# Attention in a decoder layer: two query tiles share an output bank, and ScalarE copies the output weights

## What is computed

```python
z = jnp.einsum('bhqd,bhkd->bhqk', qi, kf) * scale
causal = key_pos[None, :] < q_pos[:, None]
log_1m_beta = jnp.where(causal, jax.nn.log_sigmoid(-z), 0.0)
stick = lax.cumsum(log_1m_beta, axis=3, reverse=True) - log_1m_beta
a = jnp.where(causal, jnp.exp(jax.nn.log_sigmoid(z) + stick), 0.0)
return jnp.einsum('bhqk,bhkd->bhqd', a, vf)
```

## Time and profile before

| | us |
|---|---|
| median of three runs | 2598.17 |
| the profiled execution | 2601.36 |
| its span | 2599.7 |
| attention, from the first scores to the last addition | 435.1 to 945 |
| busy in the whole span: PE, DVE, ACT, POOL | 2402.9, 1651.4, 1229.3, 737.2 |

### The profile page before, as it was taken

One profiled execution on the slowest core, in us unless ns is written; L12 is line 12 of the kernel. 1 busy time (PEld: TensorE's weight loads), 2 busy tenths in 40 slices (PEclk: granted clock), 3 DMA queues, 4 the chain that ended last, 5 costly groups with the idle time before them and its releaser, 6 DMA issues. The chain is left out here.

```text
span 2599.7 us, 38083 instructions
## 1 busy us (share of the span) xinstructions
PE 2402.9 (92%) x11925; PEld 2004.6 (77%) x11925; DVE 1651.4 (64%) x2100; ACT 1229.3 (47%) x2065; POOL 737.2 (28%) x624
## 2 busy tenths in 40 slices
PE   6989997989999979985999999799999899999997
PEld 5767885878888868873888888688888687878785
DVE  4424222989999967865777777877777634343433
ACT  4311112879898955544444444544444324232322
POOL 0000001776666634554222222222222001010101
PEclk9999998999999989997999999899999999999998
DMA  7922335243343125774322223432222254545452
GB/s 238 285 72 80 129 121 147 70 125 98 93 98 89 45 86 176 230 226 155 98 73 92 77 79 109 145 96 74 85 84 73 80 180 148 191 142 194 149 194 105
DMA packets 283122, 326.90 MB, mean 126 GB/s; under 512 B 11972, under 2 KB 217468, under 8 KB 278396
## 3 DMA queue, kind: packets, MB, share of 16 engines
q1 hardware_dynamic: 278396, 308.68, 39.0%
q0 software_dynamic: 4608, 16.78, 1.6%
HBM read 216.36 MB, written 92.27 MB: 119 GB/s over the span
## 5 line engine op out<-in xcount | busy, mean ns | idle before, releaser
L747 POOL TENSOR_TENSOR weight<-beta,stick 128x512 f32<-128x512 f32 (+3 forms) x320 | 304.2, 958 | 586.4 <-ACT beta L696 467.3
L794 DVE TENSOR_TENSOR_SCAN stick<-z_ps,stick,beta 128x512 f32<-128x512 f32 x192 | 245.1, 1276 | 13.8 <-ACT z_ps L697 12.7
L511 PE MATMUL out_ps<-hT,w_hi 128*128 128x512 f32 x768 | 239.5, 393 | 10.0 <-DVE w_lo L445 10.0
L1638 PE MATMUL value_chain_ps<-wide,wu_hi 128*128 128x512 f32 x704 | 219.9, 394 | 16.8 <-DVE up_cols L1587 9.7
L696 ACT ACTIVATE beta<-z_ps 128x512 f32<-128x512 f32 (+3 forms) x320 | 171.1, 535 | 70.7 <-PE z_ps L828 61.1
L1418 ACT ACTIVATE wu_hi<-wu_sums 128x512 fp32r<-128x512 f32 x175 | 110.4, 633 | 186.9 <-PE value_chain_ps L1638 93.0
L1755 POOL TENSOR_TENSOR y<-y,x 128x1024 f32<-128x1024 f32 x16 | 38.9, 2432 | 505.6 <-DVE y L1814 505.4
L845 PE MATMUL wT_ps<-ident,weight 128*128 128x128 f32 x1088 | 174.7, 276 | 5.7 <-POOL weight L747 5.7
L511 PEld LDWEIGHTS out_ps<-hT,w_hi 128*128 128x128 f32 x768 | 144.9, 189 | 42.1 <-DVE w_lo L445 10.4
L697 ACT ACTIVATE z_ps<-z_ps 128x512 f32<-128x512 f32 (+3 forms) x320 | 172.2, 538 | 0.0
L1638 PEld LDWEIGHTS value_chain_ps<-wide,wu_hi 128*128 128x128 f32 x704 | 133.8, 191 | 45.9 <-DVE wu_lo L1515 10.0
(11 more groups left out here) (210 smaller groups left out, 6236.8 us busy)
## 6 DMA issues: line engine op xcount, KB each, us to landing
wu_f<-in_w_down SPq DMA_DIRECT2D x88, 512.0 KB, 3.6
wu_f<-in_w_up SPq DMA_DIRECT2D x44, 512.0 KB, 5.0
bridge<-in_w_up SPq DMA_DIRECT2D x44, 512.0 KB, 5.0
f_scratch<-f SPq DMA_DIRECT2D x44, 512.0 KB, 2.6
wu_sums<-f_scratch SPq DMA_DIRECT2D x88, 256.0 KB, 3.8
x_scratch<-x SPq DMA_DIRECT2D x56, 256.0 KB, 2.6
xt<-in_x SPq DMA_DIRECT2D x16, 512.0 KB, 5.8
hT<-h_hi SPq DMA_DIRECT2D x16, 512.0 KB, 4.5
```

The source lines that it names most:

```text
L511: m = pe.matmul(out_ps[half + j][:, :], w[slot][:, k, :], hT[h][:, k, j * BANK:(j + 1) * BANK], start=(k == 0 and t == 0), stop=(k == kc - ...
L747: pool.tensor_tensor(weight[v % weight_ring][:, 0:w], beta[v % stick_in][:, 0:w], stick[q % 2][:, at:at + w], ALU.mult).then_inc(weight_do ...
L794: dve.tensor_tensor_scan(stick[q % 2][:, at:at + w][:, ::-1], backwards, beta[u % stick_in][:, 0:w], start, ALU.mult, ALU.bypass).then_inc ...
L1638: m = pe.matmul(bank[:, :], w[left][:, k, :], x[right][:, k, :], start=(not adds and k == 0 and t == 0), stop=(k == half - 1 and t == 2), ...
```

## The change

The two output buffers get twice the width, 128 x 2 x 2 x 128, which is a whole bank each: one buffer holds two neighbouring query tiles. PE asks for a free buffer only at even tiles, counted in pairs, and DVE adds only after odd tiles, with one instruction that reads 512 elements and writes 256. The wait for the stored `mixed` of the pair of heads before moves from tile 0 to tile 1. SP counts 8 additions in a head in place of 16.

`high_wo` goes from DVE to ACT and becomes an activation with the function Copy, at the head of the step, ahead of the two sigmoids. `wo_part` now gives units 8, 12, ..., 68 of the first pair, for ACT and for POOL's `low_wo`, which stays the same otherwise. SP's code for the weights is not changed.

```diff
-        o_ps = [n.ps(f"o_ps{i}", [P, 2, P]) for i in range(2)]
+        o_ps = [n.ps(f"o_ps{i}", [P, 2, 2, P]) for i in range(2)]
...
         def wo_part(i, u):
-            m = (u - per_head) // 2
-            return m if isinstance(i, int) and i == 0 and (u - per_head) % 2 == 0 and 0 <= m < 2 * a["kc"] else None
+            m = (u - lead) // 4
+            return m if isinstance(i, int) and i == 0 and (u - lead) % 4 == 0 and 0 <= m < 2 * a["kc"] else None
...
-                    sp.wait_ge(o_read, done((pair * 2 + e + 1) * tiles - 1, lead))
+                    sp.wait_ge(o_read, done((pair * 2 + e + 1) * (tiles // 2) - 1, lead))
...
+                def high_wo(m):
+                    k, h = m // 2, m % 2
+                    act.wait_ge(wo_in[h], 16 * (k + 1))
+                    act.activation(wide[h][:, k, :], wo_f[:, h, :], ACT.Copy).then_inc(wo_hi_done, 1)
                 def step(i, u, behind):
+                    if wo_part(i, u) is not None:
+                        high_wo(wo_part(i, u))
                     if u < total:
...
-                def high_wo(m):
-                    k, h = m // 2, m % 2
-                    dve.wait_ge(wo_in[h], 16 * (k + 1))
-                    dve.tensor_copy(wide[h][:, k, :], wo_f[:, h, :]).then_inc(wo_hi_done, 1)
                 def step(i, u, behind):
-                    if wo_part(i, u) is not None:
-                        high_wo(wo_part(i, u))
...
-                    if behind(read_lag) and units[behind(read_lag)[0]][5]:
+                    if behind(read_lag) and units[behind(read_lag)[0]][5] and units[behind(read_lag)[0]][1] % 2 == 1:
...
-                        if q == 0:
+                        if q == 1:
                             dve.wait_ge(mixed_out[e], stored(i if u >= read_lag else i - 1, 32))
-                        dve.tensor_reduce(mixed[e][:, q * P:(q + 1) * P], o_ps[q % 2][:, :, :].rearrange("e h k -> e k h"), AX.X,
-                                          ALU.add).then_inc(o_read, 1)
+                        dve.tensor_reduce(mixed[e][:, (q - 1) * P:(q + 1) * P].rearrange("e (q k) -> e q k", q=2),
+                                          o_ps[q // 2 % 2][:, :, :, :].rearrange("e q h k -> e q k h"), AX.X, ALU.add).then_inc(o_read, 1)
...
-                    if first:
-                        pe.wait_ge(o_read, freed(i * (2 * tiles) + (e * tiles + q), 2, lead))
+                    if first and q % 2 == 0:
+                        pe.wait_ge(o_read, freed(i * tiles + (e * (tiles // 2) + q // 2), 2, lead))
```

More of the change, by code:

```diff
@@ L854, in values @@
                         for b in range(per):
-                            m = pe.matmul(o_ps[q % 2][:, 0, :], v_f[:, key // P + b, :, :], wT_f[whole_before[u] % wT_ring][:, b, :],
+                            m = pe.matmul(o_ps[q // 2 % 2][:, q % 2, 0, :], v_f[:, key // P + b, :, :], wT_f[whole_before[u] % wT_ring][:, b, :],
                                           start=False, stop=False, skip_group_check=True)
@@ L861, in values @@
                     closes = last or (key == BANK and whole[u + 1])
-                    if first:
-                        pe.wait_ge(o_read, freed(i * (2 * tiles) + (e * tiles + q), 2, lead))
+                    if first and q % 2 == 0:
+                        pe.wait_ge(o_read, freed(i * tiles + (e * (tiles // 2) + q // 2), 2, lead))
                     for b in range(w // P):
-                        m = pe.matmul(o_ps[q % 2][:, :, :], v_both[e][:, key // P + b, :, :], wT[halved_before[u] % wT_ring][:, b, :, :],
+                        m = pe.matmul(o_ps[q // 2 % 2][:, q % 2, :, :], v_both[e][:, key // P + b, :, :], wT[halved_before[u] % wT_ring][:, b, :, :],
                                       start=(first and b == 0), stop=(closes and b == w // P - 1))
```

## The result

The changed kernel takes 2609.85 us, the median of six runs (2607.42 to 2613.56), against 2598.09 for the kernel before (2595.36 to 2602.58). The ratio is 1.0045, with a 95% interval of 1.0033 to 1.0056: slower by 11.7 us. The profiled execution took 2613.56 us, its span is 2611.8.

A forecast was written before the change was run, and what follows sets the result against it. In an attention head no engine is far behind: PE 60.28 of 64 us, DVE 59.53, ACT 56.44. Terms 21.6 - 3.7 + 2.5 + 4 - 11.3 - 5 = +8.1 us on 2598.2 give 2606.3, range 2595 to 2618.

The forecast's parts named there:

- The wait on the first weight transfer: First pair's first head, unit 8: ACT stands until the first weights land at 468.2 us, +21.6 us.
- The clock: After the stall at unit 8, TensorE's clock falls to 0.50: +2.5 us, from +1.3 to +4.
- its term of -3.7: First head after unit 8: POOL's wait for that head's last load and the clock dip are over by 468 us, -3.7.
- The ACT copies: First pair: fifteen more ACT weight copies cost between 0 and 0.5 us each, taken +4 us (0 to 8).
- The second head: First pair's second head returns to an undisturbed one, without DVE copies, crowded POOL or late loads: -11.3 us (to -7).
- The addition: Attention heads: one DVE add for two query tiles saves queue time and PE waits, -5 us (0 to -12).
- only some of it returns: Of PE's 10.5 us of waits for a reduction, only part comes back, since DVE's scan is late next.
- The other heads: Sign in the new profile: heads outside the first pair shorter by 0.3 to 1 us.
- The overlapped price: DVE in a full queue: one 512 add takes 0.58 us against 2 x 0.31, saving 0.04 per pair, 2.6 us.
- The first rival: The add pays in full, -13 us in place of -5, and the copies hide (+2): 2596 us, chance 17%.
- The second: ACT becomes the bound of the first pair, copies and POOL's subtraction show, clock stays low: +19.6 us, 2618, chance 18%.
- The third: The first weight transfer lands before ACT asks, before about 449 us, so no stall: -13 us, 2585, chance 6%.

The follow-up runs named there:

- late copies: Changed kernel with weight copies and POOL subtractions at units 24, 27, ..., 69 of the first pair in place of 8, 12, ..., 68: 2591.23 us, ratio 0.9970.
- early transfers: Changed kernel with the second head's loads issued between weight transfers 1 and 2 in place of ahead of transfer 0: 2599.97 us, ratio 1.0005.
- copies off DVE: Kernel before with the weight copies on ACT at their old units 40, 42, ..., 70: 2591.72 us, ratio 0.9976.
- addition alone: Kernel before with only the output banks and joint addition changed, weight copies still on DVE at units 40, 42, ..., 70: 2600.93 us, ratio 1.0006.

## Why the prediction was right, and where not

The direction, the size and the path through the stall were right: 2606.3 was forecast, 2609.85 measured, inside the range.

- **The wait on the first weight transfer: right to 1 us.** 446.00 + 22.2 to landing became 447.55 + 23.4. The idle time was to be about 21 us and is 21.89; with the copy, unit 8 was to come 21.6 us late and comes 22.6. It was readable because the row of before holds the landing of a transfer for which nobody waited. The late copies (0.9970 in place of 1.0045) and the early transfers (1.0005) settle it from two sides.
- **The clock: it fell as forecast, its price is not shown alone.** The granted clock is 0.50 to 480 us, and units 8 to 16 take 14.8 us after the stall, against 12.5 in an undisturbed head: 2.3 us, where 2.5 were taken. But POOL's queue has a part in them. The prediction held the work on the first head's values for over by 468 us (its term of -3.7); POOL makes `v_f` only at 472.89 us, for 2.36 us, is busy 5.00 of 5 us in 475 to 480, and both PE (1.34 us) and ACT (1.09 us) wait for its weight. No run parts the two, so the size may be luck.
- **The ACT copies: too dear.** 4 us were taken. From unit 16 to the end the first head is 1.0 us longer than an undisturbed one, and the second not at all (61.6 against 62.0). 128 further ACT copies cost 2.6 us, 0.02 each, where 0.25 each were taken. Those copies are of 256 elements, 0.30 us each in a full queue, against 0.5 for a weight copy.
- **The second head: right in size, its causes only in part.** -11.3 was taken and -11.7 measured. The text named DVE's copies, POOL's subtractions at every second unit and the late loads, without a price for each. The copies off DVE return 7.4 us, the late loads are some 3 us, and POOL's subtractions by themselves 1 us at most.
- **The addition: wrong.** -5 us was taken for it, in a range from 0 to -12. Its term is zero in the change within some 3 us (1.0044 without it, 1.0045 with it), and 4 to 5 us of loss beside late copies. The step that failed is "only some of it returns" of the 10.5 us of PE waits: none did, as the wait moved to DVE's low half, while the text had expected the scan to be what comes next. The other heads were to be 0.3 to 1 us shorter each, and are not (364.9 and 365.2 us for the six). The overlapped price held: 0.664 us of busy time and 0.58 to the next start. By the 63% at which DVE work shows, 2.6 to 3.8 us of saved queue time are worth about 2 us by estimate; that the larger block takes them back is argued, not shown.
- The first rival is out: the addition alone gives a ratio of 1.0006, not 0.9968 or less, so the 8.4 us of recorded busy time are not what the removed instructions are worth. The Trainium skill (VectorE: DVE Perf Modes, The DRAIN you can't avoid) says what that rival cites, but the same section adds that a next op that is not held starts earlier. The trace fits that addition: the scan at 748.27 starts 0.08 us before the recorded end of the reduction ahead of it. The second is out by the second head. The third is out: the first weight transfer landed at 470.95 us, behind the last load of the second head (470.3).

The forecast change was 8.1 us, that of the spans is 12.1. The 4.0 between them, by the table: +1.0 to unit 8, -1.2 for the rest of the first head and -2.4 for the second (the copies, less any share of the addition that had been meant for these heads), +5.3 for the addition and the later pairs, +1.3 outside attention. Two wrong terms of opposite sign, copies and addition, cancel in part, and the sum is better than its parts.

## What to carry to other kernels

When a step is moved earlier, look up when its data land in the trace of before, not when they are issued: a transfer that nobody waits for hides how late it is. Count everything that stands behind the waiting instruction on its engine. And value a saved instruction by the distance to the next start in a full queue, then by how much of added work on that engine shows in the time.

## What was not expected of the hardware

DVE paced the heads with 59.5 us busy of 64, below PE's 60.3, and yet only 63% of added DVE work showed (50 to 75%). PE, busy 94% of a head by its rows, took 256 more transposes at a price of 8.8 us out of 28. DVE's copy of 128x512 took 0.649 us on average beside POOL's subtraction at every second unit, with single ones from 0.399 to 1.390, while ACT's copy of the same rows took 0.62 to 0.72 in the changed kernel.
